# Two landing slots instead of three for the second layer's weight units, with two expert transfers moved forward

## The chip, the cores and the metric

One NeuronCore of a Trainium2 chip runs the whole program. The metric is the device time of one execution in microseconds; times of several runs are given as their median.

## The reference

Two transformer blocks on a sequence of 256 tokens, width 1024, float32, and a final RMS norm. The first block mixes a windowed pooling branch, a stick-breaking attention and a cross attention on a memory, and ends in a gated feed-forward layer. The second ("hybrid layer") has two attentions (block-sparse and top-k), gates, an output projection, and then a mixture of experts:

```python
def hybrid_layer(x, ...):
    h = rms_norm(x, g_mix)
    qa, ka, va, qb, kb, vb, qi, ki, wi, ga, gb = jnp.split(h @ w_in, SPLIT_POINTS, axis=-1)
    ...
    mixed = sigmoid(ga) * (o_a @ w_proj_a) + sigmoid(gb) * (o_b @ w_proj_b)
    x = x + mixed @ w_out
    x = x + hier_moe(rms_norm(x, g_ffn), w_group, b_group, w_expert, b_expert, w1, w3, w2)
    return x

# hier_moe: each token picks one of 4 groups and 2 of its 8 experts; each of the 32 experts is
hid = jax.nn.silu(xb @ w1[e]) * (xb @ w3[e])     # w1, w3: 1024 x 512 float32, 2 MB each
y = hid @ w2[e]                                  # w2: 512 x 1024 float32, 2 MB
```

## The kernel before

**Units.** All dense weights of both blocks are cut into 96 units of 1 MB (128 partitions x 2048 float32). A unit goes through three places: SP loads it into a landing slot (`ring`, three slots of 8 KB per partition, unit u in slot u % 3); ACT writes the rounded high part `w_hi` of it (line 1391), DVE the rest `w_lo` = slot minus high part (line 1697), and PE multiplies both. `w_hi` and `w_lo` have three places of their own. `hi_ready` and `lo_ready` count the units split so far; `unit_done` counts the units that PE has finished. ACT splits unit u when its load has landed and unit u-3 is off PE; a slot is free again when DVE's subtraction has read it. So `load(u)` waits for `lo_ready` at u-2 (unit u-3 is split).

Units 65 ("kiwi") to 95 are the second layer's. Units 66 to 79 are projections (units 66 to 71 and 74 to 77 are followed by rotary embeddings, whose additions on DVE count `rope_done`), 80 to 87 gates with the attention heads worked between, 88 to 91 the merge (`second_merge` is 88), 92 to 95 the output projection (`out20` is 92), with the residual added into `h` by DVE (line 2098) and turned over by PE (line 942) for the routing.

**Experts.** Each expert has three 2 MB matrices: `w1` (gate), `w3` (up), `w2` (down). They land in SBUF regions that the dense stage frees: `arena` has 12 blocks of 8 KB per partition; the ring is blocks 1 to 3; `odd_w` is blocks 10-11 (w1), 0-1 (w3) and 2-3 (w2); `even_w` blocks 8-9 (w1), the place of `x_both` (w3) and blocks 4-5 (w2); `third_w` takes the first two places of the split weights (w1, w3) and blocks 6-7 (w2), `fourth_w` the places of `o_hi` (w1) and `h` (w3), and for w2 that of `even_w`, which the first expert must have left. Expert e uses `even_w`, `odd_w`, `third_w`, `fourth_w` for e = 0, 1, 2, 3; later experts alternate. PE works experts in order, three matrices each: 128 small matmuls for w1 and w3 (line 1328), 32 for w2 (line 1344).

**Order of loads.** All of these transfers are issued by one engine, SP, in program order; a wait holds back everything behind it. In the dense stage SP's loop runs over the units, with halves of the first expert's matrices between them. After the last unit's load it goes on by hand:

```python
        sp.wait_ge(unit_done, out20)
        expert_load(3, fourth_w, 0, in_fourth[0])
        sp.wait_ge(sum_T, 8)
        expert_load(1, odd_w, 0, landed_w[1][0])
        sp.wait_ge(lo_ready, U - 2)
        expert_load(1, odd_w, 1, landed_w[1][1])
        sp.wait_ge(unit_done, U - 2)
        expert_load(2, third_w, 0, in_third3[0])
```

The ACT and DVE orders around the last units: units 93 and 94 are split only in the step of unit 92, after the merge's sums (`sum_hi`, `sum_lo`) have been taken; unit 95 is split in the step of unit 93, ahead of that step's additions into `h`.

Of the kernel before, what the change touches and what calls it, by code (L numbers as in the profile page):

```python
# [24 lines left out]
F32 = mybir.dt.float32  # L25
F32R = mybir.dt.float32r
I32 = mybir.dt.int32
ACT = mybir.ActivationFunctionType
# [3 lines left out]
P = 128  # L32
T = 256
TB = T // P
D = 1024
# [6 lines left out]
UC = 256  # L42
# [6 lines left out]
EXPERTS = GROUPS * PER_GROUP  # L49
EFF = 512  # L50
SLOTS = 32
# [238 lines left out]
def layers_kernel(nc, a, table, windows, out):  # L290
# [146 lines left out]
    exp_out = moe("exp_out", [P, TB, 36])  # L437
    masked_e = moe("masked_e", [P, TB, EXPERTS + 6])
# [5 lines left out]
    gate_e = moe("gate_e", [P, TB, EXPERTS])  # L444
# [9 lines left out]
    hid_T = moe("hid_T", [P, P])  # L454

# [40 lines left out]
    def sem(name):  # L496
        return nc.alloc_semaphore(name)
# [45 lines left out]
    landed_w = [[sem(f"{parity}_w{n}") for n in (1, 3, 2)] for parity in ("even", "odd")]  # L543
    first_half = [sem(f"first_half_w{n}") for n in (1, 3, 2)]
# [15 lines left out]


# [86 lines left out]
    def _(sp):  # L648
        def load(u):
            if u >= 3:  # L650
                sp.wait_ge(lo_ready, u - 2)
            kc, cols = units[u]["kc"], units[u]["cols"]
            dst = ring[:, u % 3, 0:kc * cols].rearrange("p (c n) -> p c n", c=kc)
            for c0, c1, src in units[u]["src"]:
                sp.dma_start(dst[:, :, c0:c1], src).then_inc(landed[u % 3], 16)
# [46 lines left out]

        for u in range(S2 + 3 * (NF - 2), U):
            if u == second_merge + 1:
                sp.wait_ge(o_done, 20)
                half_load(0, 0)
            elif u == second_merge + 2:
                half_load(0, 1)
            elif u == second_merge + 3:
                sp.wait_ge(unit_done, second_merge)  # L710
                half_load(1, 0)
            elif u == out20:
                half_load(1, 1)
            load(u)
            if u in (out20, out20 + 1):
                if u == out20:
                    sp.wait_ge(o_done, 28)
                half_load(2, u - out20)
# [4 lines left out]
        sp.wait_ge(lo_ready, U - 2)  # L723
        expert_load(1, odd_w, 1, landed_w[1][1])
# [7 lines left out]
        expert_load(2, third_w, 2, in_third3[2])  # L732
        sp.wait_ge(route_T, 4)
# [10 lines left out]
        expert_load(3, fourth_w, 2, in_fourth[2])  # L744
# [105 lines left out]
    def _(pe):  # L850
# [409 lines left out]
        def quad_body(q):  # L1260
# [56 lines left out]
            for e in range(QUAD):  # L1317
                places, landing, arrived = place_of(e)
                done = pe.snap(e0 + e) if looped else e0 + e
                for n in range(2):  # L1320
                    if not looped and e == 0 and (q == 0 or n == 0):
                        pe.wait_ge(first_half[n], 16 * (q + 1))
                    pe.wait_ge(landing[n], arrived)
# [18 lines left out]
                for b in range(4):  # L1342
                    for g in range(4):
                        last = mm(ps[SLOTS * g:SLOTS * g + SLOTS, 7, 0:UC],  # L1344
                                  hid_T[:, SLOTS * b:SLOTS * b + SLOTS], places[2][:, b, UC * g:UC * g + UC],
                                  start=b == 0, stop=b == 3, tile_position=(0, SLOTS * g))
# [12 lines left out]
    def _(act):  # L1359
# [25 lines left out]
        def split_one(u):  # L1385
            x = units[u]
            n = x["kc"] * x["cols"]
            if u >= 3:
                act.wait_ge(unit_done, u - 2)
            act.wait_ge(landed[u % 3], landings(u))  # L1390
            fn(w_hi[:, u % 3, 0:n], ring[:, u % 3, 0:n], ACT.Copy).then_inc(hi_ready, 1)  # L1391
# [285 lines left out]
    def _(dve):  # L1677
# [16 lines left out]
        def split_one(u):  # L1694
            n = units[u]["kc"] * units[u]["cols"]
            dve.wait_ge(hi_ready, u + 1)
            v.tensor_tensor(w_lo[:, u % 3, 0:n], ring[:, u % 3, 0:n], w_hi[:, u % 3, 0:n].bitcast(F32),  # L1697
                            ALU.subtract).then_inc(lo_ready, 1)
# [640 lines left out]
```

## Time and profile before

| what | value |
|---|---|
| median of 3 runs | 1076.98 us (1076.45 to 1077.9) |
| the profiled execution | 1077.02 us |
| its span, first to last instruction | 1074.8 us |
| PE busy | 925.6 us, 86% |
| DVE, ACT busy | 502.5 us (47%), 365.5 us (34%) |
| HBM read | 308.15 MB, mean 288 GB/s with the 1.05 MB written |

Busy time of PE is the time in which a matmul runs; the DMA share is the mean busy share of the core's 16 DMA engines in a stretch. The span is cut into stretches: the dense part ends at about 622 us, the routing at about 631, the experts' matmuls begin at 634.9 and end at about 1065.

### The profile page before, as it was taken

How to read it: one execution, taken by the hardware profiler on the slowest of the kernel's cores; microseconds unless marked ns; L12 is line 12 of the kernel's file. 1: busy time of each engine (PE TensorE's matmuls, PEld its weight loads, DVE VectorE, ACT ScalarE, POOL GpSimd, SP SyncE). 2: the span in 40 equal slices, each digit the busy share in tenths (PEclk: the TensorE clock that was granted, in tenths of full speed). 3: DMA queues.
4: the chain of work that ended last, by engine and by line, in shares of the span. 5: the costliest groups of instructions: out<-in, count | busy, mean ns of one | idle time of the engine just before them, and what ended most of it. 6: DMA issues, size and time to landing. Idle time of an engine off the chain costs nothing.

```text
span 1074.8 us, 22602 instructions
## 1 busy us (share of the span) xinstructions
PE 925.6 (86%) x9976; PEld 763.6 (71%) x9976; DVE 502.5 (47%) x806; ACT 365.5 (34%) x518; POOL 30.5 (3%) x34
## 2 busy tenths in 40 slices
PE   9999999999999999999999988786657667676764
PEld 8998877888888888989777876664545445454542
DVE  4746768687676667889877651110000100010101
ACT  6445765454444345444666330010000000000001
POOL 0200002110000001000000000000000000000000
PEclk9999999999999999999999999998998978898987
DMA  9954434545655644544457999999999999999994
GB/s 330 309 181 163 154 131 155 181 153 196 195 188 166 215 154 157 158 157 157 157 186 285 391 420 424 425 426 425 427 429 429 429 427 427 428 427 429 429 428 186
DMA packets 86285, 309.99 MB, mean 288 GB/s; under 512 B 5580, under 2 KB 46232, under 8 KB 73432
## 3 DMA queue, kind: packets, MB, share of 16 engines
q1 hardware_dynamic: 84560, 304.72, 73.5%
q0 software_dynamic: 1056, 4.20, 1.2%
q8 instruction: 42, 0.69, 0.3%
q10 hardware_dynamic: 616, 0.28, 0.1%
q14 instruction: 11, 0.09, 0.0%
HBM read 308.15 MB, written 1.05 MB: 288 GB/s over the span
## 4 chain that ended last, share of the span: by engine, by line
PE 58%; issue 38%; DVE 1%; ACT 1%; DMA 1%; POOL 0%; SPq 0%; POOLq 0%; DVEq 0%; ACTq 0%
PE ps L855 13%; PE ps L857 12%; PE ps L856 12%; PE ps L974 8%; PE ps L976 4%; PE ps L1328 1%; PE ps L1122 1%; PE ps L1110 1%; DMA arena<-in_w_in 1%; PE ps L1344 1%; PE ps L1272 0%; PE ps L949 0%; PE ps L1084 0%; DVE h L1784 0%; PE ps L1083 0%
## 5 line engine op out<-in xcount | busy, mean ns | idle before, releaser
L1328 PE MATMUL ps<-arena,xg 128*32 128x128 f32 x2816 | 110.4, 322 | 75.3 <-DMA arena<-in_w 71.2
L1697 DVE TENSOR_TENSOR w_split<-arena,w_split 128x2048 fp32r<-128x2048 f32 x70 | 159.3, 2287 | 30.1 <-ACT w_split L1391 29.6
L1328 PEld LDWEIGHTS ps<-arena,xg 128*32 128x32 f32 x2816 | 94.4, 130 | 93.8 <-DMA arena<-in_w 85.2
L2274 DVE TENSOR_TENSOR hid<-silu_e,ps 128x128 f32<-128x128 f32 x32 | 12.1, 378 | 315.8 <-ACT silu_e L1651 315.8
L1391 ACT ACTIVATE w_split<-arena 128x2048 fp32r<-128x2048 f32 x70 | 132.8, 1900 | 66.2 <-PE ps L857 57.8
L974 PE MATMUL ps<-x_both,w_split 128*128 128x512 f32 x352 | 124.6, 398 | 0.8 <-DVE x_both L1792 0.8
L855 PE MATMUL ps<-w_split,x_both 128*128 128x512 f32 x256 | 101.9, 398 | 0.9 <-DVE w_split L1748 0.9
L856 PE MATMUL ps<-w_split,x_both 128*128 128x512 f32 x256 | 99.8, 390 | 0.0
L857 PE MATMUL ps<-w_split,x_both 128*128 128x512 f32 x256 | 99.8, 390 | 0.0
L976 PE MATMUL ps<-x_both,w_split 128*128 128x256 f32 x352 | 98.8, 281 | 0.0
L1651 ACT ACTIVATE silu_e<-ps 128x128 f32<-128x128 f32 x32 | 8.9, 277 | 245.2 <-PE ps L1328 245.2
L1344 PE MATMUL ps<-arena,hid_T 128*32 128x256 f32 x960 | 64.5, 409 | 27.7 <-DMA arena<-in_w 27.0
L974 PEld LDWEIGHTS ps<-x_both,w_split 128*128 128x128 f32 x352 | 66.1, 188 | 17.0 <-issue 1.0
L855 PE MATMUL ps<-x_both,w_split 128*128 128x256 f32 (+1 forms) x256 | 73.0, 285 | 0.8 <-DVE x_both L1792 0.8
L857 PE MATMUL ps<-x_both,w_split 128*128 128x256 f32 (+1 forms) x256 | 72.3, 283 | 0.0
L856 PE MATMUL ps<-x_both,w_split 128*128 128x256 f32 (+1 forms) x256 | 72.3, 283 | 0.0
L1344 PEld LDWEIGHTS ps<-arena,hid_T 128*32 128x32 f32 x960 | 31.6, 115 | 55.0 <-issue 32.7
L855 PE MATMUL ps<-w_split,o_hi 128*128 128x512 f32 (+1 forms) x176 | 68.2, 387 | 0.5 <-DVE gates L1911 0.5
L1707 DVE TENSOR_TENSOR w_split<-arena,w_split 128x2048 fp32r<-128x2048 f32 x24 | 55.0, 2293 | 26.3 <-ACT w_split L1401 25.3
L857 PE MATMUL ps<-w_split,o_lo 128*128 128x512 f32 (+1 forms) x176 | 67.1, 381 | 0.0
L856 PE MATMUL ps<-w_split,o_hi 128*128 128x512 f32 (+1 forms) x176 | 67.0, 380 | 0.0
L976 PEld LDWEIGHTS ps<-x_both,w_split 128*128 128x128 f32 x352 | 66.5, 189 | 0.4
(318 smaller groups left out, 1460.0 us busy)
## 6 DMA issues: line engine op xcount, KB each, us to landing
arena<-in_w SPq DMA_DIRECT2D x71, 2048.0 KB, 26.1
arena<-in_w_in SPq DMA_DIRECT2D x41, 1024.0 KB, 5.2
even_w<-in_w SPq DMA_DIRECT2D x13, 2048.0 KB, 27.3
arena<-in_w_ffn_in SPq DMA_DIRECT2D x22, 1024.0 KB, 5.0
third_w<-in_w SPq DMA_DIRECT2D x6, 2048.0 KB, 15.8
arena<-in_w_ffn_out SPq DMA_DIRECT2D x11, 1024.0 KB, 4.9
arena<-in_w_out SPq DMA_DIRECT2D x8, 1024.0 KB, 6.8
arena<-in_w SPq DMA_DIRECT2D x6, 1024.0 KB, 7.1
```

What stands on the lines that cost most here:

```text
L855: mm(dst, l_hi, r_hi, start=start, stop=False)
L856: mm(dst, l_hi, r_lo, start=False, stop=False)
L857: return mm(dst, l_lo, r_hi, start=False, stop=stop)
L974: mm(ps[:, bank + n, :], hi[:, c, col], x_both[:, c, :, :].rearrange("p a b -> p (a b)"), start=c == 0, stop=False)
L976: last = mm(ps[:, bank + n, 0:T], lo[:, c, col], x_hi[:, c, :], start=False, stop=c == kc - 1)
L1110: last = nc.tensor.transpose(m[:, P * t:P * t + P], src[:, P * t:P * t + P], ident)
L1328: last = mm(ps[SLOTS * g:SLOTS * g + SLOTS, 6, P * n:P * n + P], xg[:, c, SLOTS * e:SLOTS * e + SLOTS], places[n][:, c, P * g:P * g + P], ...
L1344: last = mm(ps[SLOTS * g:SLOTS * g + SLOTS, 7, 0:UC], hid_T[:, SLOTS * b:SLOTS * b + SLOTS], places[2][:, b, UC * g:UC * g + UC], start=b ...
L1391: fn(w_hi[:, u % 3, 0:n], ring[:, u % 3, 0:n], ACT.Copy).then_inc(hi_ready, 1)
L1697: v.tensor_tensor(w_lo[:, u % 3, 0:n], ring[:, u % 3, 0:n], w_hi[:, u % 3, 0:n].bitcast(F32), ALU.subtract).then_inc(lo_ready, 1)
L1707: v.tensor_tensor(w_lo[:, s, :], ring[:, s, :], w_hi[:, s, :].bitcast(F32), ALU.subtract)\
L2274: v.tensor_tensor(hid[:, :].rearrange("p (b i) -> p i b", b=4), silu_e[:, :].rearrange("p (i b) -> p i b", b=4), ps[:, 6, P:2 * P].rearran ...
```

## The change

From unit 67 on (`last_three`), units land in two slots, ring slots 1 and 2 in turn (`ring_of`), and a load waits for the split of the last unit that lay in its slot (`slot_given_up`). Up to unit 68 the waits stay as they are. Ring slot 0, arena block 1, is thus free once unit 66 is split. The second expert's up matrix (`odd_w` w3, blocks 0 and 1) is now loaded in two halves of 1 MB, the first after load 72 and a wait for `rope_done` 4, the second after load 74; its load at the end of the dense stage goes. A new tile `spare_w2` takes the first of four blocks (512 KB) of the fourth expert's down matrix, issued right after the third expert's down matrix; the other three quarters keep their place in the queue. Room for it comes from `gate_e`, which now lies where `masked_e` lies. PE gets two waits for the new landings.

```diff
-    gate_e = moe("gate_e", [P, TB, EXPERTS])
+    gate_e = moe("gate_e", [P, TB, EXPERTS], where=masked_at)
+    spare_w2 = moe("spare_w2", [P, D])
...
+    last_three = next(u for u, x in enumerate(units) if x["name"] == "kiwi") + 1
+    last_three += (1 - last_three) % 3
+
+    def ring_of(u):
+
+        return u % 3 if u < last_three else 1 + (u - last_three) % 2
+
+    def slot_given_up(u):
+
+        return next(v for v in reversed(range(u)) if ring_of(v) == ring_of(u)) + 1
...
-                sp.wait_ge(lo_ready, u - 2)
+                sp.wait_ge(lo_ready, slot_given_up(u))
-            dst = ring[:, u % 3, 0:kc * cols].rearrange("p (c n) -> p c n", c=kc)
+            dst = ring[:, ring_of(u), 0:kc * cols].rearrange("p (c n) -> p c n", c=kc)
...
+        def odd_half(half):
+
+            part = slice(4 * half, 4 * half + 4)
+            sp.dma_start(odd_w[1][:, part, :], sources[1][:, 1, part, :]).then_inc((odd_first, landed_w[1][1])[half], 16)
...
             load(u)
+            if u == last_three + 5:
+                sp.wait_ge(rope_done, 4)
+                odd_half(0)
+            elif u == last_three + 7:
+                sp.wait_ge(lo_ready, last_three)
+                odd_half(1)
...
         expert_load(1, odd_w, 0, landed_w[1][0])
-        sp.wait_ge(lo_ready, U - 2)
-        expert_load(1, odd_w, 1, landed_w[1][1])
...
         expert_load(2, third_w, 2, in_third3[2])
+        sp.dma_start(spare_w2[:, :], sources[2][:, 3, 0, :]).then_inc(spare_in, 16)
...
         sp.wait_ge(e_y, 1)
-        expert_load(3, fourth_w, 2, in_fourth[2])
+        sp.dma_start(fourth_w[2][:, 1:4, :], sources[2][:, 3, 1:4, :]).then_inc(in_fourth[2], 16)
...
+                    if not looped and q == 0 and (e, n) == (1, 1):
+                        pe.wait_ge(odd_first, 16)
...
+                    w2_block = places[2][:, b, :]
+                    if not looped and q == 0 and (e, b) == (3, 0):
+                        pe.wait_ge(spare_in, 16)
+                        w2_block = spare_w2[:, :]
...
-            fn(w_hi[:, u % 3, 0:n], ring[:, u % 3, 0:n], ACT.Copy).then_inc(hi_ready, 1)
+            fn(w_hi[:, u % 3, 0:n], ring[:, ring_of(u), 0:n], ACT.Copy).then_inc(hi_ready, 1)
...
-            v.tensor_tensor(w_lo[:, u % 3, 0:n], ring[:, u % 3, 0:n], w_hi[:, u % 3, 0:n].bitcast(F32),
+            v.tensor_tensor(w_lo[:, u % 3, 0:n], ring[:, ring_of(u), 0:n], w_hi[:, u % 3, 0:n].bitcast(F32),
```

## Rows read from the trace of the kernel before

**Rows 1.** The page's 40 slices of 26.9 us: rate of DMA traffic.

```profile
GB/s 330 309 181 163 154 131 155 181 153 196 195 188 166 215 154 157 158 157 157 157 186 285 391 420 424 425 426 425 427 429 429 429 427 427 428 427 429 429 428 186
```

**Rows 2.** Windows of all engines: stretch, length, busy times, PE clock, DMA share, GB/s.

```profile
430.00:560.00 130.00, 130.00 (x825) 110.49 (x824) 112.45 (x232) 67.25 (x105) 0.00 (x0) 1.00 0.48 155
...
596.00:598.00 2.00, 2.00 (x14) 1.79 (x13) 1.89 (x3) 1.56 (x3) 0.00 (x0) 1.00 1.00 250
598.00:604.00 6.00, 6.00 (x30) 4.92 (x30) 5.32 (x5) 4.79 (x4) 0.00 (x0) 1.00 0.91 369
604.00:619.00 15.00, 15.00 (x79) 12.69 (x78) 7.26 (x8) 3.31 (x7) 0.00 (x0) 1.00 1.01 425
...
640.00:1056.00 416.00, 285.89 (x6064) 221.19 (x6056) 38.48 (x103) 29.15 (x76) 0.59 (x1) 0.89 1.01 427
```

**Rows 3.** Groups of instructions, 660 to 1056 us: the largest group.

```profile
L1328 PE MATMUL ps<-arena,xg 128*32 128x128 f32 x2560 | 100.9, 323 | 70.9 <-DMA arena<-in_w 68.8 <-issue 2.1
```

**Rows 4.** Timeline of SP's queue, 575 to 640 us: start, length, transfer issued.

```profile
583.10 6.18 SPq L655 DMA_DIRECT2D arena<-in_w_out  x2
596.00 0.34 SPq L694 DMA_DIRECT2D extra_w<-in_w  x1
600.04 1.97 SPq L694 DMA_DIRECT2D arena<-in_w  x2
608.26 0.33 SPq L694 DMA_DIRECT2D third_w<-in_w  x1
...
614.64 8.09 SPq L694 DMA_DIRECT2D third_w<-in_w  x2
625.90 0.33 SPq L694 DMA_DIRECT2D extra_w<-in_w  x1
636.02 1.25 SPq L701 DMA_DIRECT2D arena<-in_w  x2
```

**Rows 5.** DMA issues: 430-530, at 513.4, 596.0, 600.0, 601.6, 608.3, 622.4; us to landing last.

```profile
arena<-in_w_in SPq DMA_DIRECT2D x16, 1024.0 KB, 5.1
...
arena<-in_w_in SPq DMA_DIRECT2D x1, 1024.0 KB, 5.5
...
extra_w<-in_w SPq DMA_DIRECT2D x1, 2048.0 KB, 8.3
...
arena<-in_w SPq DMA_DIRECT2D x1, 2048.0 KB, 9.4
...
arena<-in_w SPq DMA_DIRECT2D x1, 2048.0 KB, 13.3
...
third_w<-in_w SPq DMA_DIRECT2D x1, 2048.0 KB, 11.6
...
third_w<-in_w SPq DMA_DIRECT2D x1, 2048.0 KB, 12.1
```

**Rows 6.** Timeline of DVE, 577 to 612 us: units 92 to 94, the residual.

```profile
586.60 2.29 DVE L1697 TENSOR_TENSOR w_split<-arena,w_split 128x2048 fp32r<-128x2048 f32 x1 [1.19 <-ACT w_split L1391]
...
599.36 4.49 DVE L1697 TENSOR_TENSOR w_split<-arena,w_split 128x2048 fp32r<-128x2048 f32 x2 [0.68 <-ACT w_split L1391]
...
606.99 0.68 DVE L2098 TENSOR_TENSOR h<-h,ps 128x512 f32<-128x512 f32 x1
```

**Rows 7.** Timeline of PE, 600 to 636 us: the residual's first turn within unit 94.

```profile
609.43 0.60 PE L942 MATMUL ps<-tab,h 128*128 128x128 f32 x4
```

**Rows 8.** Timeline of ACT, 440 to 530 us: high parts of units 73, 75, 83.

```profile
452.00 1.90 ACT L1391 ACTIVATE w_split<-arena 128x2048 fp32r<-128x2048 f32 x1
...
465.76 1.91 ACT L1391 ACTIVATE w_split<-arena 128x2048 fp32r<-128x2048 f32 x1 [3.82 <-PE ps L857]
...
513.93 1.92 ACT L1391 ACTIVATE w_split<-arena 128x2048 fp32r<-128x2048 f32 x1 [2.94 <-PE ps L857]
```

**Rows 9.** Timeline of DVE, 440 to 512 us: rotary addition, split of unit 81.

```profile
446.77 0.69 DVE L1955 TENSOR_TENSOR kb<-head_expo,head_right 128x512 f32<-128x512 f32 x1
...
507.19 2.29 DVE L1697 TENSOR_TENSOR w_split<-arena,w_split 128x2048 fp32r<-128x2048 f32 x1
```

More of the change, by code:

```diff
@@ L437, in layers_kernel @@
     exp_out = moe("exp_out", [P, TB, 36])
+    masked_at = mo
     masked_e = moe("masked_e", [P, TB, EXPERTS + 6])
@@ L543, in layers_kernel @@
     landed_w = [[sem(f"{parity}_w{n}") for n in (1, 3, 2)] for parity in ("even", "odd")]
+    odd_first, spare_in = sem("odd_w3_first_half"), sem("spare_quarter_in")
     first_half = [sem(f"first_half_w{n}") for n in (1, 3, 2)]
@@ L1342, in quad_body @@
                 for b in range(4):
+                    w2_block = places[2][:, b, :]
+                    if not looped and q == 0 and (e, b) == (3, 0):
+                        pe.wait_ge(spare_in, 16)
+                        w2_block = spare_w2[:, :]
                     for g in range(4):
                         last = mm(ps[SLOTS * g:SLOTS * g + SLOTS, 7, 0:UC],
-                                  hid_T[:, SLOTS * b:SLOTS * b + SLOTS], places[2][:, b, UC * g:UC * g + UC],
+                                  hid_T[:, SLOTS * b:SLOTS * b + SLOTS], w2_block[:, UC * g:UC * g + UC],
                                   start=b == 0, stop=b == 3, tile_position=(0, SLOTS * g))
```

## The prediction

> **What bounds the kernel now.** I read the page's slices first [rows 1]: DMA traffic climbs to 420 GB/s in the slice at 618 us and stays between 420 and 429 until the last slice. The windows say how full that is [rows 2]: from 640 to 1056 us the DMA share is 1.01 at 427 GB/s, while PE is busy 286 of 416 us. The groups of that stage name the wait [rows 3]: PE idles 68.8 us before its largest group, and it waits for landings. So the expert stage is a stream of weights, and the end is when the stream ends plus a tail. Every 2 MB block (2.097 MB) costs 2.097/427 = 4.91 us; a 512 KB quarter costs 1.2 us.
>
> The question is then where the saturated stream begins. In the windows it is 598 us: 596 to 598 drops to 250 GB/s, 598 to 604 has 369, from 604 on it is 425 [rows 2]. The queue's timeline shows why: the last units' loads go out at 583.10 to 589, and the next transfer, fourth expert's gate matrix (`expert_load(3, fourth_w, 0)`), is issued at 596.00 [rows 4]. Before that, from 430 to 560 us, the share is 0.48 and PE is 130 us busy in 130 [rows 2]: bytes moved there are free, and they are what the change is after.
>
> **The change, part by part.** The sum is made against the profiled execution, 1077.0 us (span 1074.8 plus 2.2 around it); the median of the runs shown is 1076.98, the same.
>
> *Bytes taken out of the stream.* The second expert's up matrix (2 MB) goes out during units 72 and 74: -4.9 us. The quarter of the fourth's down matrix only changes place within the saturated stream (before 636 us instead of after 642 us), and the queue is not empty at either place: the transfer issued at 625.90 is at least 4.9 us behind the one issued at 622.4, which lands at 634.5 (12.1 us later, [rows 5]), so it lands at 639.4, 3.4 us after the next issue at 636.02 [rows 4]. Bytes that wait in a queue that never empties are worth 0. Even the missing 2 MB leaves room for an idle queue at 636, and the quarter fills that; it would count only then.
>
> *The wait that grows.* With three slots, `load(u)` waits until unit u-3 is split; with two, until u-2 is. For unit 95, the last, `slot_given_up(95)` is 94: the split of unit 93. On DVE [rows 6] unit 92's split ends at 588.9 (start 586.60, 2.29), and that is when load 95 goes out now. Units 93 and 94 are split back to back from 599.36 in 4.49 us, the first done at 601.66. So load 95 moves from 588.9 to 601.7. Load 94 moves from 583.1 to 588.9 and loses nothing, since DVE comes to its split only at 601.6.
>
> *What is queued behind it.* SP is one queue. Behind load 95 stands `expert_load(3, fourth_w, 0)`, issued at 596.00 now [rows 4], and after it `expert_load(1, odd_w, 0)`, from 600.04. They go out at 602.1 and 602.5. DMA has meanwhile run dry: load 94, issued at 588.9, lands by about 595. A 1 MB load on an idle queue lands after 5.1 us (median of 16), at most 5.5 [rows 5], so load 95 lands at 606.9; in between, some 8 us have next to no traffic where before there were 2.
>
> *The new start of the stream.* Now: issue 596.00, landing after 8.3, at 604.3; the second 2 MB (600.04 + 9.4) at 609.4; the third, which the change removes (601.6 + 13.3), at 614.9; third expert's gate matrix (608.26 + 11.6) at 619.9 [rows 4, 5]. After: 606.9, then two blocks at the pace of 4.9 to 5.5 that the intervals above show. I take the two measured ones, 5.2 and 5.5, since both orders begin on a queue that was idle: 617.6; then the third expert's gate matrix 4.9 later, 622.5. That is 2.6 us later than 619.9. With 4.9 for all it is +1.8; with load 95 landing after 5.5 and a first interval of 5.9 (596.00's own block landed 8.3 after issue, 0.7 more than 5.1 + 2.45) it is +3.6. In one line: the removed bytes give 4.9 and the delayed start takes 7.5.
>
> The Trainium skill, DMA: Bandwidth & Descriptors (Anatomy of one DMA), fits a transfer as 2.0 us plus bytes/436 GB/s, 4.4 us for 1 MB. By it load 95 would land 0.7 us earlier and the sum be +1.9; the rows have 5.1, so they decide.
>
> *Does the queue then stay full to the end?* The issues at 608.26 stay. Those at 614.64, 622.4 and 625.90 wait for PE, and PE gets later: load 95 lands at 606.9, ACT's copy ends at 608.9, DVE's split (2.29) at 611.2 instead of 607.0, and DVE's additions into `h`, which stand behind it at 606.99 [rows 6], start at 611.1. PE turns `h` over within unit 94 at 609.43 [rows 7] and needs the first of them, ready at 611.8: a stall of 2.4 us. Unit 95's own weights are in time (611.2 against 617). So the third's up matrix goes out at 617.0, its down matrix at 624.8, the fourth's up matrix at 628.3 and the fifth's first half at 638.4. When they go out, the transfers already queued land until 627.4, 632.3, 638.4 (with the quarter) and 643.3. Each issue is 4.9 us or more ahead of the end of the queue: no gap. The 2.4 us of PE are hidden under the stream, which is itself later. If the stream weren't later they would be on the path.
>
> *Other edits.* Two more waits on PE (`odd_first`, `spare_in`) are for data landed at least 10 us earlier: 0. `gate_e` in place of `masked_e` adds no instruction: 0; its cover is DVE's program order. Two more issues on SP at 0.5 us each, one at 448, one at 625, stand before waits: 0 to 0.3. Splitting into 1 MB and 0.5 MB pieces costs nothing in a full queue.
>
> The Trainium skill, SBUF — State Buffer (The DMA setup-cost knee), speaks against small pieces: each pays a fixed 2 us. For three more pieces that would be up to 6 us if each stood alone; behind others the stream keeps 425 to 427 GB/s, so I leave it out.
>
> *The dense stage.* The tightest place is unit 73: SP waits for `rope_done` 4, DVE's addition into `kb` at 446.77 + 0.69 [rows 9], sends the 1 MB half at 447.5 and load 73 at 447.9, which lands at about 455.5 instead of before 452.00, when ACT splits it [rows 8]. ACT is 3.5 us late, DVE about 3, the split is done at 461.7; PE starts unit 73 at 465.7 (ACT's split at 465.76 waits for that same end of unit 72, [rows 8]). Slack 4 us: 0. Elsewhere a load has from the end of split u-2 to ACT's start on u, and that is shortest for units 81 to 83: split 81 ends at 509.5, ACT starts on 83 at 513.93 [rows 8, 9], 0.7 us less than 5.1, while DVE comes to split 83 only at 520: hidden by 4 us of slack. Bounds: 0 to +2.
>
> Sum: 1077.0 - 4.9 + 7.5 + 0 = **1079.6 us**.
>
> **Rivals.**
> 1. *Faster: the start isn't lost.* If the first expert transfers went out near 596 as now (SP freed early, or DMA's dry time shorter because the unit loads of 577 to 589 spread into it), the 4.9 us would come through, less 0.9 where the queue has then run dry at 608.26 (that block alone lands after 5.1 + 2.45, at 615.8, against 614.9): 1073.0 us. The decisive point is whether the transfer now issued at 596.00 goes out before 598. Against it: the wait stands ahead of it in SP's order, and ACT's `sum_hi` work, not a load, sets 599.36. 0.1.
> 2. *No difference.* The start of the stream is +1.8 or less and some later hole of the old stream is filled: 1077 to 1079. The old stream's first 6 us ran at 369 GB/s, which is 0.8 us of missing bytes [rows 2], and the last windows are full; so there is little to fill. 0.2.
> 3. *Slower than the sum: PE in the dense stage stalls too.* The 3.5 us delay at unit 73, or ACT and DVE late at units 81 to 83 where the landing is up to 0.8 us late, reach PE. Everything behind moves by that amount: 1081.5 to 1083. PE had no idle time there, so any stall counts fully. 0.12.
> The forecast itself, start of stream later and queue full afterwards, 0.58.
>
> **How the numbers follow.** What a measurement here can tell is 0.2%, 2.2 us: below 1074.8 is faster, above 1079.1 slower. The forecast's own range is 1078.8 to 1080.6 (+1.8 to +3.6), about four fifths of it above 1079.1. Slower: 0.58 x 0.8 + 0.12 + a part of case 2's upper edge = 0.63. Faster 0.10. Same 0.27. The range must leave out no more than 0.2: case 1 and the upper part of case 3 fall outside, so 1076.6 to 1082.0.
>
> **What the profile after would show.** Right: SP's timeline has a 1 MB issue at 601 to 602 and then two of 2 MB within 1 us; windows show the stretch 596 to 603 nearly empty; DVE's last split ends near 611; PE has a stall of 2 to 3 us around 610 and its first expert matmul comes 2 to 3 us later than now; 640 to 1056 us keeps 427 GB/s. Step by step: PE busy 130 in 130 from 430 to 560 shows the two slots are enough there. Wrong would be: an issue of 2 MB at 596 (case 1), a hole in the stream near 636 (then the quarter and PE's delay count), or PE idle before 580 (case 3).

## The result, and the profile after

| | before | changed |
|---|---|---|
| median | 1077.21 us (1076.45 to 1077.9, 4 runs) | 1084.46 us (1080.71 to 1086.05, 4 runs) |
| ratio | | 1.0059, 95% interval 1.0044 to 1.0073 |
| profiled execution, its span | 1077.02, 1074.8 us | 1080.71, 1078.4 us |

The changed kernel is slower, as forecast, but by 7.25 us where 2.6 were forecast, and outside the range. It was timed beside the kernel before four times in all: medians 1084.46, 1081.57, 1081.33 and 1082.03. The 23 executions behind them (4, 6, 6 and 7) run from 1080.05 to 1086.05, median 1082.03; those of before, in six comparisons, from 1075.98 to 1081.98 with medians of 1076.88 to 1078.01. The first comparison is thus the highest of four, and the other three differ from before by 4.2, 3.3 and 5.2 us.

The profile after: first the page's slices (rate of DMA traffic) and the packets, MB and share of the queue that fetches instructions; the kernel before has the same 42 packets. They answer to [rows 1]:

```profile
GB/s 330 306 181 165 152 132 153 183 149 195 194 194 169 218 141 116 206 186 162 153 228 286 281 413 425 402 428 425 425 430 428 430 429 429 428 428 428 428 428 212
...
q8 instruction: 42, 0.69, 0.3%
```

The slice at 593 us fell from 391 to 281 GB/s, and the one at 674 us from 425 to 402. The windows say where (columns as in [rows 2]):

```profile
430.00:560.00 130.00, 129.77 (x824) 110.01 (x824) 111.50 (x233) 67.62 (x105) 0.00 (x0) 1.00 0.53 176
590.00:596.00 6.00, 6.00 (x30) 4.96 (x29) 3.26 (x6) 0.60 (x1) 2.58 (x2) 1.00 0.86 325
596.00:603.00 7.00, 7.00 (x38) 5.90 (x37) 5.12 (x7) 5.18 (x5) 0.00 (x0) 1.00 0.01 4
603.00:606.00 3.00, 3.00 (x14) 2.45 (x14) 2.57 (x2) 0.00 (x0) 0.00 (x0) 1.00 0.58 195
606.00:619.00 13.00, 10.96 (x57) 8.97 (x56) 6.81 (x7) 4.49 (x7) 0.00 (x0) 1.00 1.03 436
640.00:1056.00 416.00, 291.49 (x6191) 226.01 (x6194) 42.87 (x122) 29.43 (x77) 0.59 (x1) 0.89 1.01 426
```

Seven microseconds at 4 GB/s stand where before moved 250 and 369 GB/s; PE is no longer busy all of 430 to 560; and it is 2 us short in 606 to 619. SP's timeline shows the cause of the empty stretch, beside [rows 4]:

```profile
590.03 13.13 SPq L670 DMA_DIRECT2D arena<-in_w_out  x2
603.20 0.51 SPq L709 DMA_DIRECT2D extra_w<-in_w  x1
603.75 0.43 SPq L709 DMA_DIRECT2D arena<-in_w  x1
609.37 0.33 SPq L709 DMA_DIRECT2D third_w<-in_w  x1
...
629.29 0.33 SPq L709 DMA_DIRECT2D extra_w<-in_w  x1
641.04 1.25 SPq L716 DMA_DIRECT2D arena<-in_w  x2
...
676.02 0.91 SPq L709 DMA_DIRECT2D third_w<-in_w  x2
691.26 7.05 SPq L709 DMA_DIRECT2D arena<-in_w  x3
```

The first row is loads 94 and 95: 590.03 and, after the wait, 602.8. The fourth expert's gate matrix goes out at 603.20, 7.2 us later than the 596.00 of before. DVE and PE around it, beside [rows 6] and [rows 7] (idle time and its releaser in brackets):

```profile
600.47 4.49 DVE L1728 TENSOR_TENSOR w_split<-arena,w_split 128x2048 fp32r<-128x2048 f32 x2 [0.67 <-ACT w_split L1422]
...
609.80 2.29 DVE L1728 TENSOR_TENSOR w_split<-arena,w_split 128x2048 fp32r<-128x2048 f32 x1 [4.23 <-ACT w_split L1422]
612.01 0.68 DVE L2129 TENSOR_TENSOR h<-h,ps 128x512 f32<-128x512 f32 x1
```

```profile
607.85 1.92 ACT L1422 ACTIVATE w_split<-arena 128x2048 fp32r<-128x2048 f32 x1 [5.12 <-DMA arena<-in_w_out]
```

Unit 95 lands at 607.8, ACT copies, DVE subtracts until 612.1, and only then adds into `h`. PE, which turns `h` over within unit 94, waits 2.04 us for it:

```profile
612.74 0.66 PE L967 MATMUL ps<-tab,h 128*128 128x128 f32 x4 [2.04 <-DVE h L2129]
```

In the stage of the stream the largest group still waits for landings, as in [rows 3]:

```profile
L1355 PE MATMUL ps<-arena,xg 128*32 128x128 f32 x2511 | 98.8, 323 | 70.8 <-DMA arena<-in_w 69.2 <-issue 1.6
```

Landings (an issue's start plus its time to landing) give the account of the profiled executions: third expert's gate matrix 619.8 before and 623.8, 624.6, 624.3, 625.7 in the four profiles of the changed kernel; last weights 1061.5 before and 1065.0, 1066.9, 1066.4, 1066.9; from there to the end 13.3 us, in one of them 14.9.

### The profile page after: what moved, and what is told of

The parts are those of the page before. It is cut to its first block, busy times and chain, and to the rows that moved or that the text cites. A ratio compares the mean times of both kernels' runs of the same rounds, so it can differ in the third digit from the quotient of the medians.

```text
span 1078.4 us, 22605 instructions
## 1 busy us (share of the span) xinstructions
PE 930.2 (86%) x9976; PEld 766.6 (71%) x9976; DVE 502.6 (47%) x806; ACT 365.7 (34%) x518; POOL 30.5 (3%) x34
## 3 DMA queue, kind: packets, MB, share of 16 engines
q0 software_dynamic: 1056, 4.20, 1.2%
## 4 chain that ended last, share of the span: by engine, by line
PE 54%; issue 39%; DVE 3%; ACT 2%; DMA 1%; POOL 0%; POOLq 0%; DVEq 0%; ACTq 0%
PE ps L880 12%; PE ps L882 11%; PE ps L881 11%; PE ps L999 8%; PE ps L1001 4%; PE ps L1355 1%; PE ps L1147 1%; ACT w_split L1422 1%; PE ps L1375 1%; DVE w_split L1728 1%; PE ps L1135 1%; PE ps L1297 1%; DMA arena<-in_w_in 0%; DMA arena<-in_w_out 0%; PE ps L1054 0%
```

## The experiments

The theory is the forecast's: load 95, late by a slot, holds SP's queue and DVE's additions, and the time is that of the stream's start. Against it stand that the stream is late for another reason (contention, the dense stage, the small pieces), and that TensorE, not the stream, sets the end. Each experiment is timed in 4 to 12 executions and compared with the kernel before on the same chip. The ratios carry 95% intervals; a difference whose interval holds 1 is not told from none. A margin below is the time that an issue has left before the stream would feel it.

### First comparison set: the start of the stream (before 1077.41 us)

**The changed kernel again.**

> The changed kernel itself, timed in five rounds. Theory S (late start of the expert stream alone, the same in every execution): all runs near the profiled 1080.7 us, within 1 us. Rival V (something in the changed kernel varies from execution to execution, and the trace caught a fast one): runs spread from 1080 to 1086 with a median near 1084.5, and the profile of a longer execution shows where the rest goes.

**The fourth expert's transfer ahead of the wait.** SP issues it before load 95's wait instead of behind it.

```diff
         for u in range(S2 + 3 * (NF - 2), U):
+            if u == U - 1:
+                sp.wait_ge(unit_done, out20)
+                expert_load(3, fourth_w, 0, in_fourth[0])
...
-        sp.wait_ge(unit_done, out20)
-        expert_load(3, fourth_w, 0, in_fourth[0])
```

> Only SP's order changes: the fourth expert's gate matrix goes out before load 95's wait. Theory S: that issue is back at 597, the stream starts at 599, the third expert's gate matrix lands 5 to 7 us earlier than in the changed kernel; PE's 2.3 us stall in unit 94 stays and now opens a hole of about 3 us at 638: 1077 to 1078 us. Rival D (it is the dense stage or the two slots that cost, not the order on SP): 1080 us or more.

**The same, and unit 95 split after the additions into `h`.** DVE no longer keeps `h` behind the late load.

```diff
-                if u not in (out0 - 1, out0 + 3, out20 - 1):
+                if u not in (out0 - 1, out0 + 3, out20 - 1, out20 + 1):
...
+                        if not half and tb:
+                            split(u + 2)
```

> As the previous one, and DVE splits unit 95 after its additions into h instead of before them. Theory S with PE's stall as second bound: the stall of 2.3 us in unit 94 is gone, the first expert matmul is at 635 to 636 us, the stream has no hole at 638, and the 4.9 us of the early matrix come through less the moved 1 MB: 1072.5 to 1074.5 us. Rival D: no better than the previous kernel, 1077 us or more.

**Two slots alone.** The up matrix is loaded late as before, and no quarter.

```diff
-            if u == last_three + 5:
-                sp.wait_ge(rope_done, 4)
-                odd_half(0)
-            elif u == last_three + 7:
-                sp.wait_ge(lo_ready, last_three)
-                odd_half(1)
...
+        sp.wait_ge(lo_ready, U - 2)
+        expert_load(1, odd_w, 1, landed_w[1][1])
...
-        sp.dma_start(spare_w2[:, :], sources[2][:, 3, 0, :]).then_inc(spare_in, 16)
```

> The two slots alone: the second expert's up matrix is loaded at the end of the dense stage as before, and the fourth's down matrix whole. Theory S: the late start costs 7.5 to 8.5 us and nothing is taken out of the stream: 1084.5 to 1086 us, 4 to 5 above the changed kernel of the same session. Rival D (the early 2 MB disturb the dense stage, the slots don't): at or below the changed kernel.

| | median us (range) | ratio [95%] | third's gate matrix lands | unit 94 on PE | issue behind the first expert's first half |
|---|---|---|---|---|---|
| before | 1077.41 | | 619.8 | 6.38 | 636.0 |
| changed | 1081.57 (1080.14 to 1082.58) | 1.0035 [1.0023, 1.0047] | 624.6 | 10.32 | 641.8 |
| fourth ahead | 1082.21 (1079.71 to 1084.74) | 1.0047 [1.003, 1.0064] | 619.9 | 10.44 | 642.5 |
| ahead, split later | 1078.52 (1076.8 to 1080.19) | 1.001 [1.0001, 1.0018] | 619.4 | 6.38 | 638.7 |
| two slots alone | 1085.0 (1084.04 to 1085.64) | 1.0068 [1.0055, 1.0081] | 628.6 | 10.65 | 640.8 |

The last three columns are of each kernel's profiled execution. The changed kernel again, from 1080.1 to 1082.6, is neither within 1 us of 1080.7, as theory S had it, nor near the 1084.5 of V. Two slots alone cost 7.6 us, and the early up matrix gives 3.4 of it back. Moving one issue ahead of the wait brings the third's gate matrix back to 619.9, and yet the time stays: the gain is lost again 25 us later. The windows (first, fourth ahead; second, with the split later) show where:

```profile
640.00:646.00 6.00, 6.00 (x180) 5.65 (x183) 3.97 (x18) 1.49 (x2) 0.00 (x0) 1.00 0.51 165
```

```profile
640.00:646.00 6.00, 5.44 (x167) 4.36 (x159) 3.09 (x12) 1.26 (x3) 0.00 (x0) 1.00 0.96 381
```

The queue has run dry because the next issue waits for PE to have done half of the first expert's gate matrix, and PE is late from unit 94. Without that stall (unit 94 back at 6.38) 3.7 us are gained. Both late things, SP's issue and DVE's addition, thus hang on load 95, and both have a price once the other is gone. The prices don't add up: the changed kernel has both, and fourth ahead, which has the stall alone, takes as long. That is what the prediction says of the 2.4 us of PE: if the stream weren't later, they would be on the path. No run has the late issue without the stall.

Both expectations for the issue ahead were missed: 1077 to 1078 us for the first and 1072.5 to 1074.5 for the second, the 4.9 us of the early matrix included. The third's gate matrix lands no more than 0.4 us earlier than in the kernel before, not 5. The second expert's gate matrix still stands behind load 95 and goes out at 602.9 and 603.2 instead of 600.04, and load 95's own 1 MB, which before landed ahead of the stream's start, now lands in it, at 607.6 and 608.9.

### Second set: the parts one by one (before 1077.72 us)

**Without the quarter; with three slots and only half the up matrix early, with and without the quarter; the quarter alone.** Three slots leave one free block (arena block 0), which takes 1 MB after unit 74.

```diff
-        sp.dma_start(spare_w2[:, :], sources[2][:, 3, 0, :]).then_inc(spare_in, 16)
```

```diff
-            if u == last_three + 5:
+            if u == 74:
                 sp.wait_ge(rope_done, 4)
                 odd_half(0)
...
+        sp.wait_ge(lo_ready, U - 2)
+        odd_half(1)
```

> The changed kernel without the spare quarter: the fourth's down matrix is loaded whole, in its old place. Theory S: the quarter only changes place in a full queue, so within 0.5 us of the changed kernel (1081 to 1082 here) and with the same spread between executions. Rival Q (the quarter and its three-quarter rest disturb the stream or cause the spread): 1079.5 us or less and a spread under 2 us.

> Three slots as before; only the first half (1 MB) of the second expert's up matrix goes early, into arena block 0, after load 74; the second half stays where the whole matrix was; the spare quarter is kept. Theory S: no late start, no stall in unit 94, 2.45 us less in the stream before 636, 1.2 of it filled again by the quarter: the fourth's up matrix lands at 638.2, the next transfer, issued at 636.0, at 641.1 after a hole of about 0.5 us: 1074.5 to 1075.5 us. Rival E (the edge at 636 takes everything: a new issue on a queue that is nearly empty costs as much as was saved): 1076.5 to 1077.5.

> As the previous one without the quarter. Theory S with the edge at 636: the queue ends 2.45 us earlier at 637, the next transfer is issued at 636.0 and lands at 641.1 as in the previous kernel, so a hole of 1.3 us opens and 1.2 us of the 2.45 come through: 1075.5 to 1076.5 us, 1 us above the kernel with the quarter. Rival (no edge, bytes are bytes): 1074.5 or less, same as or below the kernel with the quarter.

> The kernel before with the spare quarter alone: 512 KB move from behind the issue at 636 to ahead of it, in a queue that is full at both places. Theory S: 0 plus or minus 0.5 us, 1077 to 1077.9. Rival Q (small pieces cost their fixed time): 1.5 to 2 us slower; rival E (a gain of 1.2 because the queue is really empty at 636): 1076.

Changed without the quarter: 1081.72 (1081.64 to 1082.72), 1.0035 [1.0021, 1.0048], the same ratio as with it in the first set. Half early: 1077.25 (1075.8 to 1078.82), 0.9993 [0.9984, 1.0002]; half early without the quarter: 1077.12 (1075.67 to 1079.47), 0.9992 [0.9982, 1.0002]; quarter alone: 1077.64 (1076.68 to 1080.16), 0.9994 [0.9983, 1.0005]. No effect of the quarter is seen. A megabyte taken out of the stream at no cost elsewhere makes 0.5 and 0.6 us between these medians and before, and isn't told from no change; the intervals leave room for 1.9 us. Both kernels were expected to be faster than that, 1074.5 to 1075.5 and 1075.5 to 1076.5; rival E, that the issue near 636 us takes what was saved, had 1076.5 to 1077.5.

### Third set: TensorE's clock, and the ceiling of the idea (before 1078.0 us)

**The changed kernel a third time; the same with 8 dummies in unit 94's wait and 6 more in the routing's; half early with 6 more.** (A dummy is two matmul instructions; the expectations count those.) In the second profile of the changed kernel PE idles 2.15 us in unit 94 and then runs on at half the clock. Its timeline and its windows (the clock is the number behind POOL's busy time):

```profile
611.01 0.39 PE L882 MATMUL ps<-w_split,sum_lo 128*128 128x512 f32 x1
613.54 0.66 PE L967 MATMUL ps<-tab,h 128*128 128x128 f32 x4 [2.15 <-DVE h L2129]
...
615.10 0.63 PE L880 MATMUL ps<-w_split,sum_hi 128*128 128x512 f32 x1
```

```profile
614.00:616.00 2.00, 2.00 (x8) 1.57 (x7) 1.97 (x3) 1.00 (x5) 0.00 (x0) 0.57 1.11 475
```

A matmul takes 0.63 instead of 0.39 us there, until 617.6, and unit 94 takes 10.32 where the first profile has 8.65.

```diff
-CHOICE_WARM = 10
+CHOICE_WARM = 16
...
+                    if tb == 0:
+                        keep_warm(8, 5)
```

> The changed kernel once more. Theory C: after PE's 2 us stall in unit 94 TensorE's granted clock falls to 0.50 for 3.4 us in some executions (profiles: 614.3 in one, not in the other; 5.44 instead of 3.81 us for the gather of tokens at 634.5 in the other), each fall costs PE 1.6 us, and with both the next transfer is issued after the queue has run dry: runs from 1080 to 1086 us again, and this profile shows one or more spells at half clock between 610 and 660. Rival V2 (the spread is in the DMA stream alone): PE's times up to 642 us equal in all profiles.

> The changed kernel with 16 dummy matmuls (2 us) on PE where it stalls in unit 94, and 12 more (1.5 us) in the wait of the routing; both stretches are idle now. Theory C: no spell at half clock between 610 and 640, unit 94 takes 8.7 us in every execution instead of 8.7 or 10.4, median 1080 to 1081 with a spread under 2.5 us. Rival V2: no change, median 1081.5 to 1082.5 with the same spread.

> Three slots, first half of the matrix early, quarter, and the 12 more dummy matmuls in the routing's wait. If PE's chain is what decides at 636: 1075.5 to 1076.5 us, 1 us below the same kernel without them (1077.25), since falls of the clock in the routing are rarer. If not: 1077.25 plus or minus 0.5.

**The second expert's up matrix not loaded at all** (three slots, quarter; 32 KB of it keep the semaphore going, and its up product multiplies the third expert's up matrix instead, so this part of the computation is another).

```diff
-        expert_load(1, odd_w, 1, landed_w[1][1])
+        sp.dma_start(odd_w[1][:, 0:1, 0:64], sources[1][:, 1, 0:1, 0:64]).then_inc(landed_w[1][1], 16)
...
+                if not looped and q == 0 and e == 1:
+                    places = [places[0], third_w[1], places[2]]
...
+                    if not looped and q == 0 and (e, n) == (1, 1):
+                        pe.wait_ge(in_third3[1], 16)
```

> A ceiling. Three slots and the spare quarter, and the second expert's up matrix is not loaded at all in the first pass (the second expert's up product reads the third expert's up matrix, so that part of the computation is changed); 4.9 us leave the stream at no cost anywhere else. Theory E (edge: the queue ends only 3.4 us after the issue at 636, and a transfer on a dry queue needs 2.65 us more than its bytes): the fourth's up matrix lands at 635.7, the next transfer at 641.1 instead of 642.3, 1.2 us gained there and 1.2 by the quarter: 1075 us. Rival B (bytes are bytes, as in rival 1 of the prediction): 1072 to 1073 us.

Changed: 1081.33 (1080.05 to 1083.73), 1.003 [1.0018, 1.0042]. Kept warm: 1081.26 (1080.15 to 1082.33), 1.0036 [1.0022, 1.005]: the clock stays at 1.00 from 610 to 640 us, unit 94 takes 9.02, and the median does not move; it lies between what the theories C and V2 had expected. Half early, kept warm: 1077.16 (1075.79 to 1078.89), 0.9995 [0.9986, 1.0004], where 1075.5 to 1076.5 was expected if PE's chain decides. The half clock in unit 94 is real and isn't what sets the level. No up matrix at all: 1077.82 (1075.26 to 1078.88), 0.9993 [0.9984, 1.0002], where 1075 was expected. Two megabytes less at no cost at all, and the kernel isn't seen to be faster. The third's gate matrix lands at 616.7, 3.1 us earlier, and the fourth's up matrix at 639.03, 0.4 earlier than before; the issue behind it comes from PE at 638.0 and lands 5.1 us after it, as a lone one does. The 4.9 us go at the issues that wait for an engine: the blocks issued at 608.68, 622.82 and 638.0 land 6.5, 5.7 and 4.1 us after the one before, where a full queue makes 4.9, 4.9 and 2.45.

### Fourth set: what a late TensorE costs (before 1076.88 and 1078.01 us)

**Dummy matmuls ahead of the first expert's gather, 22 and 50 in the changed kernel, 22 in the kernel before; the changed kernel beside them; then 11 in each.**

```diff
+            if not looped and q == 0:
+                keep_warm(22, 5)
             if not looped:
                 pe.wait_ge(n3_ready, 2)
```

> The changed kernel with 22 more dummy matmuls on TensorE ahead of the first expert's gather: by the 0.12 us of one dummy in the trace TensorE is 2.4 us late from there, nothing else is moved. Theory G (a lateness of TensorE is hidden until the transfer issued behind the first expert's first half, 641.0 us in the changed kernel's trace, lands on an empty queue: 5.1 us after its issue against 647.7 in a full one, a margin of 1.5 us; beyond it counts one to one): +0.9 us, 1082.2 where the changed kernel beside it has 1081.3, and the interval between the landing of the fourth expert's up matrix and the next one is some 3.3 us instead of 2.5. Theory H (all hidden under the stream, as the prediction's steps say): 0, 1081.3. Theory I (every microsecond of TensorE counts): +2.4, 1083.7.

> The same with 50 dummies, 5.9 us late. Theory G: 5.9 less the margin of 1.5, +4.4, 1085.7, with a hole of about 4 us in the stream near 650 us; this would be the size of the executions at 1084 to 1086 of the first comparison. Theory H: 0. Theory I: +5.9, 1087.2.

> The kernel before with the same 22 dummies, 2.4 us late. Theory G: issue at 636.0, landing after 5.1 against 641.9 in a full queue, a margin of 0.7: +1.7 us, 1079.4 where before has 1077.7. Theory H: 0. Theory I: +2.4.

> The changed kernel as it is, beside the three above. If the 1083.8 to 1086.1 of the first comparison belong to the kernel, some of these six executions are above 1083.5; if they belonged to that comparison alone, the median is 1081.3 and the highest below 1083.8.

> The changed kernel with 11 dummy matmuls ahead of the first expert's gather, at 0.228 us each as the runs with 22 and 50 show (11.41 us for 50): TensorE is 2.5 us late from there, and the instruction queue should have its 42 packets again. Theory G (a margin of 1.5 us, beyond it one to one): +1.0 us, 1083.0 where the changed kernel has 1082.0 (four runs of 23 executions pooled), the next landing behind the fourth expert's up matrix 3.4 us after it. Theory H (hidden): 1082.0. Theory I (all counts): 1084.5.

> The kernel before with the same 11 dummies, 2.5 us late. Theory G with before's margin of 0.7 us: +1.8, 1078.9 to 1079.5. Theory H: 1077.3. Theory I: 1079.8.

| | median us (range) | ratio [95%] | over its own kernel, us |
|---|---|---|---|
| changed | 1082.03 (1080.3 to 1085.91) | 1.0045 [1.0029, 1.0062] | |
| changed, 22 | 1094.65 (1092.06 to 1096.1) | 1.0156 [1.0139, 1.0174] | +12.6 |
| changed, 50 | 1091.32 (1089.56 to 1092.62) | 1.0133 [1.0114, 1.0152] | +9.3 |
| before, 22 | 1092.93 (1092.26 to 1093.95) | 1.0143 [1.0127, 1.016] | +16.1 |
| changed, 11 | 1084.63 (1083.22 to 1084.83) | 1.0061 [1.0048, 1.0074] | +2.6 |
| before, 11 | 1080.37 (1078.21 to 1084.62) | 1.0022 [1.0011, 1.0032] | +2.4 |

The two with 11 ran later than the others, beside a before of 1078.01, without the plain changed kernel. Their 2.6 is against its 1082.03 in the table's first row; counted from the before beside each, changed with 11 is 6.6 us over, and the unaltered changed kernel 3.3 to 5.2 in its three repeats. The plain changed kernel had one execution of 1085.91, as was to be seen if the high ones are its own. The first three with dummies missed every expectation, for two reasons. A dummy is two instructions, as PE's timeline of the run with 50 has it, so it lasts 0.228 us and not 0.114:

```profile
634.92 11.41 PE L1054 MATMUL ps<-ones 128*128 128x128 f32 x100
```

and 22 of them, in either kernel, changed something at the other end of the program. The page's instruction queue of the changed kernel with 22 (packets, MB, share), its window of 800 to 1050 us, then the same window before:

```profile
q8 instruction: 88, 1.44, 0.5%
```

```profile
800.00:1050.00 250.00, 164.22 (x3396) 129.80 (x3388) 21.80 (x58) 16.63 (x43) 0.00 (x0) 0.87 1.00 423
```

```profile
800.00:1050.00 250.00, 167.22 (x3376) 127.69 (x3376) 21.55 (x58) 16.00 (x42) 0.00 (x0) 0.86 1.01 428
```

88 fetches of 16 KB instead of 42. The landings say what these cost: from 790 us on, 54 intervals in the kernel before sum to 0.02 us over 4.895 each; 56 intervals with the added fetches sum to 7.45 us over (changed) and 7.71 us (before). The window's rate shows less of it, since the fetches' own bytes are in it. The run with 50 has 43 fetches and 0.02 us. So 7.5 of the 12.6 and 7.7 of the 16.1 us are instruction fetches of the expert loop. That the loop's body came to lie across one more block of instructions is my reading of it; the count and the cost are measured.

What is left is TensorE's lateness. It shows at two places. The first is the issue behind the first expert's first half. The margin is the landing of the fourth's up matrix + 2.45 - 5.1 - that issue (2.45 us is 1 MB in a full queue, 5.1 on an empty one), the hole is the interval to the next landing less 2.45:

| profile | issue | margin | hole |
|---|---|---|---|
| changed, four profiles | 641.0, 641.8, 639.7, 642.7 | 1.5, 1.4, 3.4, 1.6 | 0.0, 0.0, 0.0, 0.4 |
| before | 636.0 | 0.7 | 0.4 |
| two slots alone | 640.8 | 4.8 | 0 |
| changed, kept warm | 639.9 | 2.8 | 0 |
| quarter alone | 636.3 | 2.3 | 0 |
| half early | 636.5 | 1.0 | 0 |
| half early, kept warm | 636.7 | 0.1 | 1.4 |
| changed without the quarter | 641.3 | -0.1 | 1.8 |
| half early without the quarter | 637.7 | -0.4 | 0.3 |
| ahead, split later | 638.8 | -0.7 | 0.9 |
| changed, 11 | 644.6 | -0.4 | 0.3 |
| up matrix not loaded | 638.0 | -1.7 | 1.6 |
| fourth ahead | 642.5 | -2.3 | 2.4 |
| before, 11 | 640.9 | -2.7 | 2.8 |
| changed, 22 | 645.8 | -3.0 | 3.9 |
| before, 22 | 642.2 | -5.5 | 6.9 |
| changed, 50 | 651.0 | -8.3 | 8.5 |

With a margin of 0.7 us or more nothing opens beyond 0.4 us; about zero the hole scatters from 0.3 to 1.8; below -1.5 it is the missing time, give or take 1.4.

The second place stands at 685 to 700 us, where after three transfers in a row (676.02 and before, in SP's timeline above) the next issue waits until PE has done the sixth expert's gate matrix. Its lead is how far ahead of the last of these landings it goes out; a 2 MB block issued on an empty queue landed after 7.9 and 8.0 us (at 596.80 and 597.10 of the two kernels with the fourth ahead) and one in a full queue lands 4.9 after the last, so by my estimate a lead under some 3 us opens a hole. Before: 5.95 us, and the next block lands 4.9 us behind the last. Changed with 11: lead 2.2, late by 2.0. Before with 11, in the profile of its slowest execution, 1084.62: lead -0.1, late by 4.7, and the window is nearly empty where before has 422 GB/s:

```profile
694.00:698.00 4.00, 4.00 (x139) 3.78 (x132) 0.13 (x1) 0.66 (x2) 0.00 (x0) 1.00 0.39 86
```

```profile
694.00:698.00 4.00, 1.55 (x56) 1.55 (x60) 0.00 (x0) 0.00 (x0) 0.00 (x0) 1.00 0.99 422
```

The unaltered changed kernel has leads of 4.8, 4.1, 4.3 and 3.6 us there, and its block is late by 0.6, 1.0, 1.0 and 1.6. A hole that PE opens explains little of it. Fourth ahead and quarter alone have leads of 3.8 and 4.2 and are on time; and before is late by 1.3 one block further on, at a lead of 7.3, so that the lateness against it is gone with the next landing. In both late intervals the queue moves its full rate, in before (first row) as in the changed kernel's fourth profile, the latest of the four (second row); in its first profile, with a share of 0.94 from 696.0 to 701.6, some 0.3 us are missing:

```profile
696.60:702.70 6.10, 5.44 (x135) 4.11 (x132) 0.69 (x2) 0.66 (x2) 0.00 (x0) 1.00 1.00 422
```

```profile
698.00:704.40 6.40, 3.58 (x92) 2.85 (x96) 0.00 (x0) 0.38 (x1) 0.00 (x0) 0.95 1.01 425
```

What 2.5 us of a late TensorE cost is 2.6 us in the changed kernel and 2.4 in the kernel before, between medians. Theory I, all of it counts, expected 1084.5 and 1079.8, theory G, only what is over the margin, 1083.0 and about 1079.2; measured are 1084.63 and 1080.37. The medians lie nearer theory I, and the holes at the second place, which G did not count, are a reason for it; but G is not ruled out, since before with 11 has the interval 1.0011 to 1.0032, 1.2 to 3.4 us, and the changed kernel's own level moves by 1.9 us from one comparison to the next. Theory H, all of it hidden, is ruled out for the kernel before, and nearly so for the changed one: its lowest execution with 11, 1083.22, is above 18 of the 23 without.

## Why the prediction was right, and where it was wrong

**The late load and the queue behind it: right.** Load 95 went out at 602.8 (forecast 601.7), the fourth's gate matrix at 603.2 (602.1), with an idle DMA in between. Against the end of unit 91 on PE, so that the dense stage is left out, the third's gate matrix lands 2.9 to 3.2 us later than before (623.8 - 597.1 against 619.8 - 596.0, and the three other profiles alike); forecast 2.6, bounds 1.8 and 3.6. By the fit of the Trainium skill, DMA: Bandwidth & Descriptors (Anatomy of one DMA), which the page gives for transfers that GpSimd issues, the estimate was 1.9. Load 95, issued by SP, landed 5.0 us after issue, nearer the row's 5.1 than the fit's 4.4.

**The dense stage at 0: the step that failed, as far as the runs show one.** It was taken as 0, bounds 0 to +2. Units 67 to 91 take 171.04 us on PE in every kernel with three slots, and 171.6 to 172.4 with two: +0.6 to +1.3, and +0.8 to +1.3 in the changed kernel's four profiles. It is the sign that rival 3 named, PE idle before 580 us. Unit 73 itself had the slack that was forecast: ACT splits it late, and PE doesn't wait. But unit 72 takes 7.3 to 7.6 us instead of 6.98 and unit 82 7.5 to 7.8 instead of 7.18; the waits named there are DVE's rotary products (`head_expo`, 0.3 us) and `head_prob` (0.2 to 0.4), which DVE comes to late. The list of PE's waits, 430 to 560 us, second profile of the changed kernel; in the kernel before the list is empty:

```profile
PE ps L1135 <- DVE head_prob L1925: 0.4, 1, 0.4
PE ps L880 <- DVE head_expo L1973: 0.3, 1, 0.3
```

With two slots alone unit 72 keeps its 6.98, so that part belongs to the early half. The forecast looked only at whether the weights were in time, not at what else DVE owes PE. No run takes DVE's lateness away by itself, so this cause is read from the waits and not tested.

**"The 2.4 us of PE are hidden under the stream": it held, with less to spare than said.** The stall came as foreseen (2.0 to 2.2 us idle in unit 94, matmul at 612.7 instead of 609.4), and was longer where the clock fell behind it: unit 94 is 8.65 to 10.33 us instead of 6.38, so 2.3 to 4.0. At the issue of 636 to 641 us it is hidden, as the margins of 1.4 to 3.4 us show. From the third's gate matrix to the last weights the four profiles lose -0.4, +0.7, +0.4 and -0.5 us against before, 0 on the mean. The forecast followed the issues to 643 us and then called the queue full to the end. At 691 us an issue again waits for PE, with a lead of 3.6 to 4.8 us where before has 5.95; it is still enough here, but a further 2.5 us isn't hidden, as the runs with 11 dummies show.

**The line "removed bytes 4.9, delayed start 7.5": about right at the start.** With two slots alone the third's gate matrix lands 8.2 us later than before, counted from the end of unit 91 (628.6 - 596.5), and the changed kernel's 2.9 to 3.2. So the delayed start takes 8.2 and the bytes give 5.0 to 5.4 there. That two slots alone cost 7.6 in the median is close to the forecast's 7.5 by luck: in its profile it is 8.2 and 0.6 in the dense stage, less 1.0 that its stream makes up later. Between the medians 3.4 is left for the bytes. With three slots half of them make 0.6 at most between medians, and all of them 0.2 in the run that loads nothing in their place. Rival 1 priced the case without a late start at 1073.0; its edge near 636 us was seen in the text for the quarter, but not carried into that price. Its like, tried with half the bytes, gives 1077.1.

**The other zeros: right.** The quarter is worth 0 as far as these medians tell (1.0035 with and without it). Its own landing comes 1.6 to 1.8 us after the one before, where its bytes make 1.2, and that of the other three quarters 3.7 to 4.0, where theirs make 3.7. So a small piece in this queue pays up to 0.6 us. The Trainium skill, SBUF — State Buffer (The DMA setup-cost knee), gives a roughly fixed 2 us for every transfer; behind others most of that doesn't show here. The added waits and `gate_e` show no wait on PE.

**The sum.** 2.6 becomes 2.9 to 3.2 for the start and 0.8 to 1.3 for the dense stage, with 0 behind them: 3.6 to 4.2 in the four profiles, about 1081 on 1077.0. The three repeats differ from before by 4.2, 3.3 and 5.2. So the mechanism was right, and of the terms of the sum the dense stage was mis-sized most. This does not explain the whole miss: the first comparison's 7.25 is some 3 us above the two terms, and where these come from stays open. Executions as high came again, 1085.91 and 1083.73 among the 19 others, so they occur in this kernel; but if the five highest fall anywhere among the 23, three or more of them are among the first four in about 1 case of 50 (an estimate), so chance is a poor account as well.

Two things that vary from execution to execution, and don't depend on the change, show in the profiles; both are the clock. One high execution was profiled, the 1083.73: its last product of expert 31 takes 3.56 us and not 1.93, at half the clock, first row here, against the first profile's, second:

```profile
1066.51 3.56 PE L1375 MATMUL ps<-arena,hid_T 128*32 128x256 f32 x32 [1.89 <-DMA arena<-in_w]
```

```profile
1065.16 1.93 PE L1375 MATMUL ps<-arena,hid_T 128*32 128x256 f32 x32 [1.88 <-DMA arena<-in_w]
```

That is 1.6 us behind the last landing, where nothing hides it; two other kernels' profiles have the same tail of 15.0 instead of 13.3 us. The other is in unit 65, the second layer's first, which takes 1.4 to 1.5 us longer in four of the 20 profiles: the changed kernel's fourth, both kernels with 11 dummies, and half early without the quarter, which has three slots. There the clock is at 0.50 behind PE's wait for the unit's inputs, as in the changed kernel's fourth profile, where the kernel before has 1.00 in the same window:

```profile
414.00:416.00 2.00, 2.00 (x11) 1.51 (x10) 1.77 (x5) 1.97 (x5) 0.00 (x0) 0.50 0.00 0
```

 No execution above 1084 of the unaltered changed kernel was profiled, so how these add up there stays open.

## What to carry to other kernels

When a wait grows, list what is issued by the same queue behind it before counting what the moved bytes give: here one landing slot less cost 7.6 us, mostly through a transfer that had nothing to do with it. Bytes taken out of a full stream can be lost again at the next issue that waits for an engine, so find every such issue up to the end, write down the margin of each, and see which engine it waits for. And when an engine gets its data late, look at everything that it owes to others in the order of its program, not only at the data.

## What the runs showed of the hardware

- Instruction fetches take time from a full stream, far beyond their bytes: 46 more fetches of 16 KB (0.75 MB, 1.8 us at 427 GB/s) made the stream 7.5 and 7.7 us later from 790 us on. In all other profiles the intervals over 4.9 us between queued 2 MB blocks lie before some 780 us, and sum to some 4 to 8 us over it; the 42 fetches end at 765 us before. That most of these are fetches too is what the run with 88 suggests; it isn't shown by itself. One is not: the block that lands at 676.8 in the kernel before, 6.0 us after the last, shares its interval with 0.44 MB of another queue.
- 22 more dummy matmuls did this (88 fetches), 11 and 50 did not (42 and 43): instructions added in one place can cost in a loop elsewhere.
- PE's granted clock fell to 0.50 (1.2 of 2.4 GHz) for some 3.4 us behind an idle time of 2 us in unit 94 in some executions and not in others, with the same code; in the last product, the same 2 us of waiting (1.88 and 1.89) ended at 1.00 in one and at 0.57 in the other (window 1066 to 1070 us), where the product takes 3.56 us instead of 1.93. In unit 65 the same happened in four of 20 profiles.
